# Gate weights and memory rows moved to later slots, the end of the mixing stage cut by token tile, the last expert's two late loads halved

## The reference

```python
h = rmsnorm(x, norm_mix)
proj = h @ w_in          # q,k,v and gates of an mLSTM, of forgetting attention (FoX), of memory attention
hm = mlstm_chunkwise(mq, mk, mv, ml_i + b, ml_f + b)     # needs the 4+4 gate columns of proj
y_fx = forgetting_attention(fq, fk, fv, fx_f + b)        # needs 8 gate columns of proj
kv = rmsnorm(mem, norm_mem) @ w_mem_kv                   # memory rows: 256 x 1024
...
merged = sum_b sigmoid(gate_b) * (y_b @ w_branch[b]);  x = x + merged @ w_out
t = rmsnorm(x, norm_moe)
logits = t @ w_router + b_router                         # top 4 of 32 experts, softmax weights
x = x + sum_e weight_e * ((clamped SwiGLU of t @ w_exp_in[e]) @ w_exp_out[e])
out = rmsnorm(x, norm_final)
```

## Time and profile before

| | us |
|---|---|
| median of 3 runs | 1351.44 (1351.33 to 1353.32) |
| the profiled execution | 1351.45 |
| its span, first to last instruction | 1349.3 |
| PE busy | 1309.5 |
| DVE busy | 468.7 |
| ACT busy | 326.8 |
| read from memory | 473.42 MB, mean 352 GB/s over the span |

### The profile page before, as it was taken

The page is one execution under the profiler, slowest core; times in us unless marked ns, Lnnn a source line. Parts: engine busy times, 40 slices in busy tenths (PEclk is TensorE's granted clock), DMA queues, the critical chain, the costliest instruction groups (busy, mean ns, idle before and its releaser), DMA issues.

```text
span 1349.3 us, 15922 instructions
## 1 busy us (share of the span) xinstructions
PE 1309.5 (97%) x6453; PEld 673.6 (50%) x6453; DVE 468.7 (35%) x801; ACT 326.8 (24%) x478; POOL 26.9 (2%) x40
## 2 busy tenths in 40 slices
PE   9999999999999999999999999999999999999996
PEld 8789888988887333333333333333333333333332
DVE  6844644445566222322232222322223222232223
ACT  5754555464344001110011000100011001010001
POOL 4000000000101000000000000000000000000000
PEclk9999999999999999999999999999999999999999
DMA  9553543537578999999999999999999999999995
GB/s 317 190 187 126 187 155 143 203 125 273 186 258 356 373 430 431 430 432 431 432 431 432 431 432 431 432 431 432 431 432 431 432 431 432 431 432 431 432 429 226
DMA packets 68377, 475.04 MB, mean 352 GB/s; under 512 B 8497, under 2 KB 10609, under 8 KB 43761
## 3 DMA queue, kind: packets, MB, share of 16 engines
q1 hardware_dynamic: 66048, 472.75, 84.6%
q10 hardware_dynamic: 2288, 1.73, 0.4%
HBM read 473.42 MB, written 1.05 MB: 352 GB/s over the span
## 4 chain that ended last, share of the span: by engine, by line
PE 85%; DMA 10%; DVE 2%; ACT 2%; issue 1%; SPq 0%; DVEq 0%; ACTq 0%
PE bank L1538 46%; PE bank L1363 17%; DMA place<-in_w_exp_in 9%; PE bank L1352 7%; PE bank L1626 4%; ACT fxqT L830 1%; PE bank L1594 1%; PE bank L1567 1%; PE bank L1551 1%; PE bank L1587 1%; PE bank L1539 1%; DMA ring<-in_w_in 1%; PE bank L1476 1%; PE bank L1495 1%; DVE w_lo L897 1%
## 5 line engine op out<-in xcount | busy, mean ns | idle before, releaser
L1538 PE MATMUL bank<-place,fxqT 128*64 128x512 f32 x1536 | 687.6, 596 | 22.0 <-ACT fxqT L830 15.5
L1539 PE MATMUL bank<-place,fxqT 128*64 128x512 f32 x1536 | 687.7, 597 | 0.0
L1538 PEld LDWEIGHTS bank<-place,fxqT 128*64 128x64 f32 x1536 | 199.3, 137 | 422.2 <-issue 390.0
L1180 DVE TENSOR_SCALAR big_a<-bank 128x512 f32<-128x512 f32 x32 | 22.1, 692 | 525.0 <-PE bank L1539 525.0
L1539 PEld LDWEIGHTS bank<-place,fxqT 128*64 128x64 f32 x1536 | 199.3, 137 | 0.0
L897 DVE TENSOR_TENSOR w_lo<-ring,w_hi 128x2048 fp32r<-128x2048 f32 x63 | 145.1, 2304 | 141.0 <-ACT w_hi L594 140.8
L594 ACT ACTIVATE w_hi<-ring 128x2048 fp32r<-128x2048 f32 x63 | 120.6, 1915 | 156.4 <-PE bank L1363 108.6
L826 ACT ACTIVATE big_a<-big_a 128x512 f32<-128x512 f32 x32 | 20.2, 630 | 435.0 <-DVE big_a L1180 435.0
L1209 DVE TENSOR_TENSOR xs<-bank,xs 128x512 f32<-128x512 f32 x132 | 81.9, 682 | 38.7 <-PE bank L1626 38.7
L1363 PE MATMUL bank<-w_hi,h_hi 128*128 128x512 f32 x224 | 88.3, 394 | 0.1
L1363 PE MATMUL bank<-w_hi,h_lo 128*128 128x512 f32 x224 | 87.3, 390 | 0.0
(11 more groups left out here) (278 smaller groups left out, 1269.7 us busy)
## 6 DMA issues: line engine op xcount, KB each, us to landing
place<-in_w_exp_in SPq DMA_DIRECT2D x128, 2048.0 KB, 27.9
place<-in_w_exp_out SPq DMA_DIRECT2D x64, 2048.0 KB, 28.2
ring<-in_w_in SPq DMA_DIRECT2D x19, 2048.0 KB, 7.7
ring<-in_w_branch SPq DMA_DIRECT2D x6, 2048.0 KB, 7.6
ring<-in_w_mem_kv SPq DMA_DIRECT2D x4, 2048.0 KB, 7.6
ring<-in_w_out SPq DMA_DIRECT2D x2, 2048.0 KB, 11.2
ring<-in_w_in SPq DMA_DIRECT2D x2, 1024.0 KB, 8.1
xs<-in_x SPq DMA_DIRECT2D x2, 512.0 KB, 4.2
```

The lines of the kernel that those rows point to most:

```text
L1180: dve.tensor_scalar(gate.rearrange("c (q p) -> c q p", q=4), bank[0][:, :].rearrange("c (p q) -> c q p", q=4), LIMIT, None, ALU.min).then_ ...
L1538: mm(o[0:CAP, :], lhsT, low, start=start, stop=stop)
L1539: return mm(o[CAP:P, :], lhsT, high, start=start, stop=stop)
```

## The change

It has three parts.

**Gates and memory later.** The six gate stages move one slot up (2, 3, 4, 5, 7, 8 become 3, 4, 5, 6, 8, 9), the memory rows' sums and scaling from slot 3 to slot 10. Of the loads, those of `wg` move behind unit 3 and are two instead of three, the memory rows' move behind unit 5.

**The end of mixing by tile.** The router's weights are multiplied once by the norm's weights (`scale_router`, DVE, slot 47), so the turned rows are plain copies. Tile 0 of the last slot is added when its part of the product is done; its last transposes stand in the middle of the last slot's second part, ACT copies them and scales both tiles. Mean square, `rstd`, top 4, mask, rank and selection are done for tile 0 and then tile 1. Fewer filling matmuls (`keep_clock`) are left.

**The last expert.** Pieces 3 and 5 of expert 31 are loaded as two halves with semaphores of their own. PE takes both parts of piece 3's first half before its second half; clamp, product, transposes and copy are done in two halves; the `put` is split around them and the selection's transposes move behind piece 4.

```diff
-_stage(2, "gate_weights")
-_stage(3, "gates")
-_stage(4, "gate_logs")
-_stage(5, "gate_sums")
-_stage(7, "gate_columns")
-_stage(8, "gate_rows")
+_stage(3, "gate_weights")
+_stage(4, "gates")
+_stage(5, "gate_logs")
+_stage(6, "gate_sums")
+_stage(8, "gate_columns")
+_stage(9, "gate_rows")
+_stage(47, "scale_router")
...
+                if halves:
+                    mid = KT // 4 * 2 * UW
+                    sp.dma_start(dst[:, 0:mid], src[:, 0:mid]).then_inc(late_in[j], 16)
+                    dst, src = dst[:, mid:], src[:, mid:]
+                sp.dma_start(dst, src).then_inc(place_in[b], 16)
...
-                if u == 2:
+                if u == RING:
...
-                if u == 1:
+                if u == RING + 2:
                     sp.dma_start(mems[:, :, :], mem[0].rearrange("(t p) d -> p t d", p=P)).then_inc(mem_in, 16)
...
-                if i == 3:
+                if i == 10:
                     square_sums(mems, 1, [mem_in, mem_in])
...
+            def deviation(t):
+                act.wait_ge(out_added, t + 1)
+                square_out(t, 1)
+                act.wait_ge(squares, 2 * TT + TT + t + 1)
+                act.wait_ge(var_ready, 1)
+                act.activation(std[:, t, 0:1], ss[:, t, 1:2], ACT.Sqrt, bias=var[:, t:t + 1],
+                               scale=1.0 / D).then_inc(std_ready, 1)
+            def scale_out(t):
+                act.wait_ge(rstd_ready, t + 1)
+                act.activation(tn[:, t, :], xs[:, t, :], ACT.Copy, scale=rstd[:, t, 0:1]).then_inc(scaled_act, 1)
...
+            deviation(0)
+            for q in (2, 3):
+                act.wait_ge(filled[4 + q], turn(4 + q, ("moe", q)))
+                act.activation(tT[:, 2 * q:2 * q + 2, 0:P], moe_turned(q, 0), ACT.Copy).then_inc(late_turned, 1)
+            scale_out(0)
+            deviation(1)
+            scale_out(1)
             warm(ACT.Exp)
...
+            score(0)
+            turn_late(2)
+            turn_late(3)
+            choose(0)
+            inverse(1)
+            score(1)
+            choose(1)
...
+                        if i == len(SLOTS) - 1 and c == 1 and kk == 2:
+                            turn_late(0)
...
+                if is_last(m, q):
+                    put(n + r, n, (0, 1))
+                    pe.wait_ge(late_act, r + 1)
...
+                    put(n + r, n, (2, 3))
+                    pe.wait_ge(late_aT, r + 1)
```

More of the change, by code:

```diff
@@ L321, in build @@
         final_ready = sem("final_ready")
+        late_in = {j: sem(f"late_in{j}") for j in (W1 - 1, PIECES - 1)}
+        late_lin, late_act, late_actT, late_aT = (sem(n) for n in ("late_lin", "late_act", "late_actT", "late_aT"))
         block = ctx.enter_context(nc.Block())
@@ L388, in load @@
             def load(e, j, b):
+                halves = isinstance(e, int) and e == NE - 1 and j in late_in
                 at = slice(e, e + 1) if isinstance(e, int) else bass.ds(e, 1)
@@ L777, in _ @@
                 if i == FIRST["out"] + 3:
-                    square_out(0)
+                    act.wait_ge(dve_drained, dve_drains(FIRST["out"] + 2))
+                    for t in range(TT):
+                        square_out(t, 0)
                 if i == FIRST["fxq"] - 1:
@@ L1114, in _, with score @@
             dve.memset(top[:, :, 8:8 + TOPK], NONE).then_inc(pads_ready, 1)
[L1115 to L1122 removed]
+            inverse(0)
+            add_out(1)
+            def score(t):
+                dve.wait_ge(rstd_ready, t + 1)
                 dve.wait_ge(logits_done, t + 1)
@@ L1211, in first_tokens @@
             def first_tokens(r):
-                select(r, 0)
-                if isinstance(r, int):
+                if not isinstance(r, int):
+                    select(r, 0)
+                else:
+                    for t in range(TT):
+                        order(t)
+                        select_tile(r, 0, t)
                     dve.wait_ge(totals_done, 1)
@@ L1417, in turn_out, with turn_late @@
                 ins.then_inc(filled[b], 1)
+            def turn_late(t):
+                pe.wait_ge(out_added, t + 1)
+                for q in (2, 3):
+                    b = 4 + q
+                    if t == 0:
+                        claim(b, ("moe", q))
+                    for c in range(2):
+                        ins = pe.transpose(bank[b][:, S * c + P * t:S * c + P * (t + 1)],
+                                           xs[:, t, P * (2 * q + c):P * (2 * q + c + 1)], ident[:, :])
+                    ins.then_inc(filled[b], 1)
             def ml_scores(h):
@@ L1587, in expert @@
                         mm(bank[5][:, :], pick_all, b2split[:, :], start=True, stop=False)
-                if not is_last(m, q):
-                    gather(n * 2 + r * 2 + 4)
-                put(n + r, n)
-                pe.wait_ge(act_ready, n + 1)
-                for g in range(4):
-                    ins = pe.transpose(bank[4][:, P * g:P * (g + 1)], act_out[:, P * g:P * (g + 1)], ident[:, :])
-                ins.then_inc(act_turned, 1)
-                pe.wait_ge(selW_ready, n * 2 + r * 2 + 2)
@@ L1610, in expert, with put @@
                     ins.then_inc(place_used[b], 1)
-                    if j == 0 and not is_last(m, q):
+                    if j == 0 and is_last(m, q):
+                        turn_weighted()
+                    elif j == 0:
                         pe.wait_ge(put_added, (n + r) * 4 + 6)
                         turn_gathered(n + 2)
-            def put(k, n=None):
+            def put(k, n=None, quarters=range(4)):
                 pe.wait_ge(selWT_ready, k + 1)
                 pe.wait_ge(yS_ready, k + 1)
-                for q, b in enumerate(PUT_BANKS):
+                for q in quarters:
+                    b = PUT_BANKS[q]
                     if n is not None and b == 0:
```

245 lines of the change are left out of this document (152 added, 93 removed).

## The result

The changed kernel takes 1354.4 us (median of 13 runs, 1352.5 to 1355.9), the kernel before beside it 1352.3 (median of 13, one of them at 1505.7, the others up to 1353.7). It is slower by 0.14 to 0.19%, where 1351.1 with a range to 1353.2 was forecast. The profiled execution takes 1355.11, its span is 1353.2: 3.9 more than before.

The account below looks back on a forecast made before the run. Time was T0 (issue of piece 10, set by PE's mixing), an unchanged DMA-bound transfer, and a tail. Terms +1.2 + 0.3 - 1.6 - 0.2 = -0.3 gave span 1349.0, plus 2.15 around it: 1351.1 us, range 1348.7 to 1353.2.

Parts of the forecast that it names:

- Gates' wait gone: In mixing, PE's wait of 2.31 us for the gates' split weights goes: -2.3.
- The new waits before slots 8 and 9: In mixing, late ACT rounding and DVE splits make PE wait 0.7 before slot 8 and 3.15 before slot 9.
- Rival (a): In mixing, the pile on DVE does not hold PE up; gates' part -2.3, time 1347.3; chance 0.11.
- Memory rows: ACT's sums in slot 10 and an extra table load delay PE by slots 12 and 13: +0.3, bounds 0 and +2.0.
- rival (b): ScalarE at slots 10 to 12: none of the sums and extra load hides, 1356.2; double-length table switch, 1355; chance 0.06.
- End by tile: At the end of mixing, the gather and the issue of piece 10 come earlier: -1.6, bounds 0 and -2.1.
- rival (c): End by tile brings nothing: ACT's second scaling, table load and exponentials delay the combination by 1.6 more; 1352.7; chance 0.13.
- SP's queue: In early loads, unit 3 no longer stands behind the small loads; no weight load was late, so nothing is won.
- Last expert: Halved piece 3 lets piece 4 start 0.6 earlier, selection's transposes cost 0.4: -0.2, bounds -1.3 and +0.5.
- The transfers behind T0: 182 expert pieces after SP issues piece 10 (T0, 443.24 before): 886 us, left alone by the change.
- The rule weighed: ScalarE table switches: 1.28 us load plus about 1.38 drain would give near 1355; the forecast followed the trace, without drain.
- +0.7 + 3.15 - 0.34 - 2.3 = +1.2: Gates' part in mixing: two new waits, less column transposes hidden in the wait (0.34) and the old wait (2.3).

Follow-up runs that it names:

- e4: The changed kernel with idle products of ones put into PE's new waits in mixing and the last expert; 1351.31 us, ratio 0.9999 to the kernel before.
- e16: e12 with six idle products of ones put between the score products at the end of mixing; 1348.97 us, ratio 0.9980 to the kernel before.
- e7: e3 with 9 idle products of ones put into PE's wait before the gates; 1349.47 us, ratio 0.9985 to the kernel before.
- e12: e10 once more, unchanged; 1350.45 us, ratio 0.9980 to the kernel before.
- e13: e8 with more idle products at the end of mixing: behind the first mask's counts and in the waits for gathered rows and bias rows; 1350.05 us.
- e18: e16 with three of its six idle products; 1348.57 us, ratio 0.9978 to the kernel before.
- e5: e3 with the last expert's pieces 3 and 5 halved; 1351.41 us, ratio 0.9999 to the kernel before.
- e14: e3 once more, unchanged; 1350.68 us, ratio 0.9985 to the kernel before.
- e1: The changed kernel with the gates' stages and weights where they were before; 1352.92 us, ratio 1.0007 to the kernel before.
- e3: The kernel before with the end of mixing by tile alone; 1349.45 us, ratio 0.9986 to the kernel before.
- e6: e3 with the memory rows at slot 10 and loaded behind unit 5; 1351.99 us, ratio 1.0001 to the kernel before.
- e11: e8 once more, unchanged; 1350.73 us, ratio 0.9984 to the kernel before.
- e10: e8 with two idle products of ones in PE's wait before the values of the mLSTM's first head; 1347.91 us, ratio 0.9967 to the kernel before.
- e8: The changed kernel with the gates' dependents spread out to slots 6, 8, 10, 11, memory rows in slot 9, last expert whole; 1351.03 us.

## Why the prediction was wrong

**The other terms held.** Gates' wait gone: yes. The new waits before slots 8 and 9 are 0.55 and, in two pieces, 2.90 from slot 8's end to slot 9's start (forecast 0.7 and 3.15); slot 9 began 1.05 later (forecast 1.2). The split for slot 9 stands behind convolution and sums, as laid out. Rival (a) fell. **Memory rows**: 0.35 against 0.3, so rival (b) fell. **End by tile**: 1.8 against 1.6, the second selection stands 1.0 behind the second mask, where the first one stood 1.6 behind it; rival (c) fell. The gathered rows did not have to be waited for longer: 0.70 in PE's bracket at 439.32, and the same before:

```profile
437.50 0.65 PE L1551 MATMUL bank<-ident,fxqT 128*128 128x128 f32 x4 [0.70 <-ACT fxqT L820]
```

**SP's queue, router's weights**: nothing, as said. **Last expert**: piece 3 is used without a wait, piece 4 starts 0.4 earlier (forecast 0.6), and the selection's two transposes, now on the path, take it back: 0.0 against -0.2. **The transfers behind T0**, put at nothing: 0.4 more, within what the traces of the other runs scatter by (888.8 to 889.8). **The rule weighed** (the Trainium skill, ScalarE: Activation LUTs, What ACT_TABLE_LOAD costs): the operation behind the load at 53.46 starts at 54.75, 0.01 behind its end, and w_hi for slot 8 at 56.80 (forecast 56.5, with 0.6 of late start here). The time that the rule would have given, 1355, is near the measured one by luck; the trace leaves as little room for a drain as before.

**The step that failed** is the sum "+0.7 + 3.15 - 0.34 - 2.3 = +1.2", and the last expert's in the same way. Both price a wait of PE at its own length and put what comes behind it at nothing. The runs showed a second price: a fall of the granted clock to 0.50 for 3.4 us behind it, 1.7 us each time, in a part of the executions. The changed kernel has waits of 0.55, 0.69 and 1.80 within 9.2 us and of 1.20 and 0.36 within 2, where before had one of 2.3 and, in the last expert, one of 1.1 and one of 0.5 seven us apart. Both of its traces have two falls: 1351.1 + 3.4 = 1354.5. The measured median is 1354.4, and e4, with the waits filled, is at 1351.3. Which falls the other runs have is not shown, and e2 (last expert whole, still 1354.4) says that it need not be these two. The range was too narrow for the same reason: none of its bounds held the clock, so 1353.2 excluded what ten of thirteen runs did. The kernel could have warned: its filling products of ones at the end of mixing are called `keep_clock` and do nothing for the result, and I priced them ("if the fillers cost nothing") without asking what they hold up.

**Of the long fall**, the two traces of the changed kernel show none. Its runs at 1355.5 and above have room for more than two short falls; whether a long one is among them, and how much of the median is owed to it, is not shown.

## What to carry to other kernels

Price a wait of TensorE twice: its length, and half of the slow stretch that can follow it. Small waits close together (0.55, 0.69 and 1.80 here) can bring one as a single wait of 2.31 can. Read the granted clock in stretches of 2 us, not in the page's forty slices, and look at several executions, since the same wait has its fall in some and not in others. Where a wait or a run of light products can't be removed, try idle products in it. Here they took 3.1 us off the changed kernel (e4), and left few longer runs where they were put among light products (e16, for 1.3 us on PE's path). They are no cure everywhere: e7, e12 and e13 gained nothing clear, and e4, e16 and e18 each kept one or two longer runs.

## What was not expected of the hardware

The granted clock fell to 0.50 behind waits that sum up to as little as 1.56 us (1.20 and 0.36 in the last expert), for 3.4 us. Behind one of 2.31 it fell for 3.4 us in the traces of e5 and e14, but not in those of before, e1, e3 and e6, which have the same wait. From within one of 5.9 it fell for 6.8 us. It also fell while PE was busy without a gap over 0.15 us, on products of 32 columns and transposes, for 6.8 us (e11) and 10.2 (e13). Six idle products (1.3 us) among them went with 1 longer run of 12 (e16), where the kernel without them had 7 of 18 (e10, e12) and with e8 and e11, 20 of 37.
